# A two-block transformer kernel: the first attention's q is squared, roped and turned in another order, and six fillings of its maxima move to two slots of the attention

## Chip, cores and metric

One Trainium2 chip, one core of it. The metric is the device time of one execution in microseconds (us); the number for a kernel is the median over its runs.

## The reference, cut to what matters here

Two transformer blocks run one after the other on 256 tokens of width 1024. The change lies in the first attention of the first block ("nsa"). Cut to what that part computes:

```
h = rms_norm(x, norm_g) * (1 + scale) + shift          # scale, shift, gate from cond @ ada_w + ada_b
q, kc, vc, ks, vs, kw, vw, gl, z = split(h @ w_in)     # q: 16 heads of 64; k, v: 4 heads
q  = partial_rope(rms_norm(q, q_g), cos, sin)
ks = partial_rope(rms_norm(ks, k_g[1]), cos, sin);  kw likewise with k_g[2]
k_cmp = partial_rope(rms_norm(compress(kc, 0), k_g[0])); v_cmp = compress(vc, 1)
gates = sigmoid(gl + gate_b)
o_cmp = softmax(q k_cmp^T * s, mask) v_cmp
o_slc = softmax(q ks^T * s, mask) vs                   # 4 blocks, all selected at 256 tokens
o_win = softmax(q kw^T * s, mask) vw
o = gates0 * o_cmp + gates1 * o_slc + gates2 * o_win
x = x + gate * ((o * silu(z)) @ w_out)
```

The softmaxes subtract the row maximum, and every matrix product is in fp32 precision. The second attention ("moba"), the first block's end and the whole second block (feed-forward, two more attentions, feed-forward) aren't touched.

## The kernel before

The program is one list of instructions per engine, written by hand as Python functions: `tensor` (PE), `scalar` (ACT), `vector` (DVE), `gpsimd` (POOL) and `sync` (SP, which issues the DMAs). Engines meet through counting semaphores: an instruction ends with `then_inc(*name(key))`, and another engine does `w.wait_ge(*name.at(key))`. Each engine runs its list in order, so a wait holds up everything behind it on that engine.

**Weights.** All weights are one stream of units of 128 x 1024 fp32 (512 KB). SP fetches unit u into one of seven buffers `w_raw`, as soon as the unit seven places earlier has been used up. ACT makes the rounded part `w_hi` (line 1028, `rounds`), DVE the remainder `w_lo = w_raw - w_hi` (line 1525, `rests`); four buffers each. PE multiplies three times per block (hi by hi, hi by lo, lo by hi), in `linear` (lines 482 and 491). The units of a second kind, "ada" (modulation weights), aren't multiplied on PE: ACT scales each half by a condition value in place (line 1032, `scale_chunk`), and POOL adds the halves up (line 2285, `sum_chunk`). An ada unit's buffer comes free when POOL has added it, and then SP fetches the unit seven places on. In the stage of z the stream takes turns: one unit of z, one of ada.

**Stages around the change, in PE's order.** The linears `nsa_q0` and `nsa_q1` (q in two halves of 8 heads, four units each, banks 0 and 1), with `compress_up(0)` between them; `compress_up(1)` (line 571); `nsa_gate` (one unit, line 491, banks 0 and 1); `nsa_vsvw` (four units, line 482, banks 2 and 3); `nsa_z0` (banks 0, 1) and `nsa_z1` (banks 2, 3), four units each, line 491; then `pair_attention`.

**How q gets ready.** After the linear, ACT squares it (`head_squares`, line 1076), DVE sums the squares (`head_sums`, line 1585), POOL takes the power -1/2 (`head_power`, lines 2257 and 2260), DVE scales q out of its bank into `tokq` (`head_scales`, line 1605), and POOL ropes it (`head_ropes`, lines 2246 to 2250). PE turns it by transposes (`q_turns`, line 506: two calls of four transposes per half), and ACT and DVE place the turned q as hi and lo parts in `qs` (`q_places`, line 1032; `q_rests`, line 1778). `k_turns`, `k_places` (kh, line 1032) and `k_rests` (kl, line 1787) do the same for k. The gate's linear waits for the scaling of q1, because both use bank 0.

**Maxima.** Softmax needs each row's maximum first. A "filling" n of 24 is a set of scores in one bank (`maxima_scores`, lines 612, 614 and 617); DVE reduces the bank to row maxima `mx` (`maxima`, line 1676), and the next filling into that bank waits for that (`filling_free`). Three fillings serve two heads. They stand behind each unit of z, three at a time: 0 to 11 under z0, 12 to 23 under z1. From filling 8 on they alternate between two banks, 7 and 4. Compressed scores (line 592, 16 matmuls) stand behind the first two units of z1; DVE masks and shifts them (`compressed_shift`, lines 1937 to 1947), ACT takes exp.

**Attention.** `pair_attention` has slots i = 0 to 7 and three more. In slot i, PE does scores (i, 0), values (i-1, 1), scores (i, 1), for odd i-2 a turn of the finished heads, then `nsa_hook(i)` and values (i, 0). Scores are lines 639 to 645, values 665 to 670. DVE does `evict(i-1)` (lines 1689 to 1703, four kinds of instruction), which waits for values (i-1, 1); values (i, 0) wait for evict's third step, `parts_of_o`. Slot i needs only the maxima of its own heads.

The banks before are set by this line, and the places where the fillings stand by the two loops over z:

```
bank = (7, 4)[n % 2] if s == "nsa" and n > 7 else order[n % 4]      # order = (7, 2, 3, 4) for nsa
...
for j in linear("nsa_z1", 1, (h_hi, h_lo), h_of(0), False, [m_reduced.at(("nsa", 6))]):
    for n in range(12 + 3 * j, 15 + 3 * j):
        maxima_scores("nsa", n, filling_free("nsa", n, first))
```

Of the kernel before, what the change touches and what calls it, by code (L numbers as in the profile page):

```python
# [188 lines left out]
def program(nc, wts, cols_d, rows_d, const_d, pos_d, gate_bias_d, x_d, out_d):  # L189
# [8 lines left out]
    with ctx:  # L198
# [203 lines left out]
        for s, per, branches, order in (("nsa", 2, slice(0, 2), (7, 2, 3, 4)), ("moba", 4, slice(0, 1), (6, 7, 4, 5))):  # L402
# [56 lines left out]
        def tensor(e):  # L459
# [308 lines left out]
            whole(linear("nsa_gate", 0, (h_hi, h_lo), h_of(0), False, [hn_scaled.at(("nsa_q1", 1, 0))]))  # L768
            for j in linear("nsa_vsvw", 1, (h_hi, h_lo), h_of(0), True, [gelu_done.at((1, 1))]):
                if j == 0:  # L770
                    compress_down(1, banks[6], heads_placed.at(("nsa_kskw", 1)))
                if j == 1:
# [4 lines left out]
                    q_turns("nsa_q0", 0, banks[5], kc_placed.at())  # L777
                if j == 2:
                    q_turns("nsa_q0", 1, banks[4], gates_done.at())
            first = {0: modulated.at((0, 3)), 1: v_done.at(("nsa", 1)), 2: v_done.at(("nsa", 1)),  # L780
                     3: heads_placed.at(("nsa_q0", 1))}
            for j in linear("nsa_z0", 0, (h_hi, h_lo), h_of(0), False, [gate_biased.at()]):
                if j == 0:
                    q_turns("nsa_q1", 0, banks[6], vc_done.at(3))
                if j == 1:
                    q_turns("nsa_q1", 1, banks[5], heads_placed.at(("nsa_q0", 0)))
                for n in range(3 * j, 3 * j + 3):
                    maxima_scores("nsa", n, filling_free("nsa", n, first))
            for j in linear("nsa_z1", 1, (h_hi, h_lo), h_of(0), False, [m_reduced.at(("nsa", 6))]):
                for n in range(12 + 3 * j, 15 + 3 * j):  # L790
                    maxima_scores("nsa", n, filling_free("nsa", n, first))
                if j < 2:
                    compressed_scores(j, (banks[5], banks[6]),
                                      (c_masked.at(0) if j else heads_placed.at(("nsa_q1", 1)),))
# [7 lines left out]
            outs = [linear("nsa_out0", 1, (o_hi, o_lo), o_two("nsa"), True, [z_done.at(("nsa_z1", 1))]),  # L802
                    linear("nsa_out1", 2, (o_hi, o_lo), o_two("nsa"), True, [exped.at(("nsa", 7, 1, 1))])]

            def nsa_hook(i):
                if i == 0:
                    compressed_turns(1, banks[0], gate_row_done.at(4))
                if i == 1:
                    ada_columns(5, banks[0], pc_done.at(1))
                if i in (4, 6, 8):  # L810
# [3 lines left out]
                if i in (9, 10):  # L814
# [3 lines left out]
                           [[m_reduced.at(("nsa", 23)), c_masked.at(1)], [m_reduced.at(("nsa", 23)), pc_done.at(0)],  # L818
# [195 lines left out]
        def scalar(e):  # L1014
# [228 lines left out]
            for j, u in enumerate(of["nsa_q1"]):  # L1243
# [19 lines left out]
            for j, u in enumerate(of["nsa_vsvw"]):  # L1263
# [7 lines left out]
                if j == 2:  # L1271
                    q_places("nsa_q0", "nsa_q", 0, banks[5])
                if j == 3:
                    q_places("nsa_q0", "nsa_q", 1, banks[4])
# [3 lines left out]
            for j, u in enumerate(of["nsa_z0"]):  # L1278
                rounds(u, 4)
                if j == 1:  # L1280
                    q_places("nsa_q1", "nsa_q", 0, banks[6])
                if j == 2:
                    q_places("nsa_q1", "nsa_q", 1, banks[5])
# [229 lines left out]
        def vector(e):  # L1513
# [401 lines left out]
            for j, u in enumerate(of["nsa_vsvw"]):  # L1915
                rests(u)
                if j == 3:
                    q_rests("nsa_q0", "nsa_q", 0, banks[5])
# [47 lines left out]
            for j, u in enumerate(of["nsa_z0"]):  # L1966
                rests(u, 4)
                if j == 0:
                    q_rests("nsa_q0", "nsa_q", 1, banks[4])
                if j == 2:  # L1970
                    q_rests("nsa_q1", "nsa_q", 0, banks[6])
                if j == 3:
                    q_rests("nsa_q1", "nsa_q", 1, banks[5])
                maxima("nsa", 3 * j, 3 * j + 1, 3 * j + 2)
            for j, u in enumerate(of["nsa_z1"]):
# [4 lines left out]
                maxima("nsa", 12 + 3 * j, 13 + 3 * j, 14 + 3 * j)  # L1980
# [5 lines left out]
            def nsa_hook(i, step_):  # L1986
# [241 lines left out]
        def gpsimd(e):  # L2228
# [322 lines left out]
```

## Time and profile before

| | |
|---|---|
| median of 3 runs | 964.97 us (962.23 to 964.99) |
| the profiled execution | 962.59 us |
| its span in the trace | 960.8 us |
| mean granted clock of TensorE | 0.979 of full |
| PE busy | 902.5 us, 94% of the span |
| DVE, ACT, POOL busy | 572.7, 489.4, 175.6 us |
| the chain that ended last | PE 84%, DVE 8%, ACT 4%, issue 2%, DMA 1%, POOL 1% |
| read from HBM | 161.37 MB, 169 GB/s over the span |

PE is busy nearly all the time, so time is to be had only where PE stands idle or where its clock is granted at half. "Busy" is the share of time with at least one instruction running, and matmuls overlap, so that the start of the next is a better measure of a matmul's cost than its duration. Times in the rows are from the start of the span.

### The profile page before, as it was taken

The page shows a single profiled execution, that of the slowest core. Times are in us where ns is not written, and L with a number is a line of the kernel's source. Part 1 is how long each engine was busy: PE and PEld are TensorE (multiplying, and loading weights), DVE is VectorE, ACT ScalarE, POOL GpSimd, SP SyncE. Part 2 cuts the span into 40 slices and gives each one's busy share as a digit, 9 for nine tenths or more (in the row PEclk, how much of TensorE's full clock was granted, in tenths as well). Part 3 has the DMA queues.
Part 4 walks back from the last instruction along what each step waited for, and adds up shares of the span by engine and source line. Part 5 has one row for each costly group of instructions (what it writes and reads, how often), then busy time and mean ns, then how long its engine had stood idle before and what let it go on. Part 6 is the DMA issues. An engine that isn't in the chain of part 4 may idle for free.

```text
span 960.8 us, 12986 instructions
## 1 busy us (share of the span) xinstructions
PE 902.5 (94%) x4989; PEld 773.8 (81%) x4989; DVE 572.7 (60%) x913; ACT 489.4 (51%) x764; POOL 175.6 (18%) x192
## 2 busy tenths in 40 slices
PE   2699898999889999999999999999999999999998
PEld 2588787899678888888888888887788788888886
DVE  5974586545766637755555446676455755555542
ACT  3334573556355564645454447585664554545431
POOL 1015344355126440000000002352001100000000
PEclk9899898999899999999999999999999999999999
DMA  9855645254646245555556655544225465555650
GB/s 359 316 183 181 219 140 190 76 149 143 199 160 196 79 142 179 175 190 195 195 184 188 176 175 188 153 140 128 67 88 157 150 206 189 175 177 187 206 176 22
DMA packets 45692, 163.26 MB, mean 170 GB/s; under 512 B 5184, under 2 KB 5440, under 8 KB 45632
## 3 DMA queue, kind: packets, MB, share of 16 engines
q1 hardware_dynamic: 45632, 162.44, 52.9%
q8 instruction: 40, 0.66, 0.3%
q14 instruction: 20, 0.16, 0.1%
HBM read 161.37 MB, written 1.05 MB: 169 GB/s over the span
## 4 chain that ended last, share of the span: by engine, by line
PE 84%; DVE 8%; ACT 4%; issue 2%; DMA 1%; POOL 1%; SPq 0%; DVEq 0%; ACTq 0%
PE bank L482 57%; PE bank L491 11%; PE bank L506 4%; DVE w_lo L1525 2%; PE bank L639 2%; DVE mx L1676 1%; DVE ada_acc L1623 1%; PE bank L645 1%; DMA w_raw<-in_weights 1%; PE bank L722 1%; PE bank L665 1%; PE bank L666 1%; PE bank L667 1%; ACT kh L1032 1%; PE bank L670 1%
## 5 line engine op out<-in xcount | busy, mean ns | idle before, releaser
L1028 ACT ACTIVATE w_hi<-w_raw 128x1024 fp32r<-128x1024 f32 (+2 forms) x249 | 259.1, 1046 | 186.0 <-PE bank L482 160.3
L1525 DVE TENSOR_TENSOR w_lo<-w_raw,w_hi 128x1024 fp32r<-128x1024 f32 (+2 forms) x249 | 303.3, 1236 | 81.3 <-ACT w_hi L1028 80.6
L482 PE MATMUL bank<-w_hi,h_hi 128*128 128x512 f32 (+1 forms) x576 | 230.5, 400 | 10.7 <-ACT h_hi L1032 6.3
L482 PE MATMUL bank<-w_hi,h_lo 128*128 128x512 f32 (+1 forms) x576 | 226.1, 393 | 0.0
L482 PE MATMUL bank<-w_lo,h_hi 128*128 128x512 f32 (+1 forms) x576 | 225.5, 392 | 0.0
L482 PEld LDWEIGHTS bank<-w_hi,h_hi 128*128 128x128 f32 x576 | 110.1, 191 | 33.6 <-issue 12.5
L482 PEld LDWEIGHTS bank<-w_hi,h_lo 128*128 128x128 f32 x576 | 109.5, 190 | 23.2
L482 PEld LDWEIGHTS bank<-w_lo,h_hi 128*128 128x128 f32 x576 | 110.2, 191 | 21.3
L2285 POOL TENSOR_TENSOR ada_acc<-ada_acc,w_raw 128x512 f32<-128x512 f32 x56 | 78.2, 1396 | 99.7 <-ACT w_raw L1032 94.4
L491 PE MATMUL bank<-h_hi,w_hi 128*128 128x256 f32 x264 | 78.8, 299 | 3.7 <-DVE tokq L1605 3.1
L491 PE MATMUL bank<-h_lo,w_hi 128*128 128x256 f32 x264 | 76.2, 289 | 0.0
L491 PE MATMUL bank<-h_hi,w_lo 128*128 128x256 f32 x264 | 76.1, 288 | 0.0
L482 PE MATMUL bank<-w_hi,a_hi 128*128 128x512 f32 x176 | 70.2, 399 | 0.0
L482 PE MATMUL bank<-w_lo,a_hi 128*128 128x512 f32 x176 | 69.3, 394 | 0.0
L482 PE MATMUL bank<-w_hi,a_lo 128*128 128x512 f32 x176 | 69.2, 393 | 0.0
L2080 DVE SCALAR_TENSOR_TENSOR act<-bank,stats,act 128x256 f32<-128x256 f32 x44 | 21.1, 483 | 67.5 <-ACT act L1395 67.5
L491 PEld LDWEIGHTS bank<-h_hi,w_hi 128*128 128x128 f32 x264 | 52.1, 197 | 4.9 <-issue 4.6
L491 PEld LDWEIGHTS bank<-h_lo,w_hi 128*128 128x128 f32 x264 | 52.2, 198 | 0.4 <-issue 0.2
L491 PEld LDWEIGHTS bank<-h_hi,w_lo 128*128 128x128 f32 x264 | 52.1, 197 | 0.0
L482 PE MATMUL bank<-w_hi,qs 128*128 128x512 f32 x128 | 44.2, 416 | 2.5 <-DVE w_lo L1525 1.8
L482 PEld LDWEIGHTS bank<-w_hi,a_lo 128*128 128x128 f32 x176 | 33.0, 188 | 8.4
L482 PEld LDWEIGHTS bank<-w_hi,a_hi 128*128 128x128 f32 x176 | 33.0, 188 | 7.7
(296 smaller groups left out, 1346.4 us busy)
## 6 DMA issues: line engine op xcount, KB each, us to landing
w_raw<-in_weights SPq DMA_DIRECT2D x298, 512.0 KB, 4.2
w_raw<-in_weights SPq DMA_DIRECT2D x4, 360.0 KB, 3.2
x<-in_x SPq DMA_DIRECT2D x1, 1024.0 KB, 7.6
gate_row<-in_gate_bias SPq DMA_DIRECT2D x2, 512.0 KB, 6.4
out<-x SPq DMA_DIRECT2D x4, 256.0 KB, 3.2
w_raw<-in_weights SPq DMA_DIRECT2D x3, 256.0 KB, 2.6
const<-in_constants SPq DMA_DIRECT2D x1, 413.5 KB, 9.0
cols<-in_columns SPq DMA_DIRECT2D x1, 208.5 KB, 2.5
```

The source lines that it names most:

```text
L482: mm = e.matmul(pb[t][:, 0:n], xs[q], ws[p], start=(k + kk == 0 and i == 0), stop=(k + kk == kts - 1 and i == 2))
L491: mm = e.matmul(o, ws[p], xs[q], start=(k + kk == 0 and i == 0 and b % 2 == 0), stop=(k + kk == kts - 1 and i == 2 and (b % 2 == 1 or b == ...
L506: mm = e.transpose(bank[0:int(np.prod(src.shape[1:])), o:o + src.shape[0]], src, ident)
L639: e.matmul(o, k[:, g, br, j * P:(j + 1) * P], qs[:, ha:hb + 1:2, j * P:S], start=m == 0, stop=False, skip_group_check=True)
L645: mm = e.matmul(o[:, a, (t - j) * P:(t - j + 1) * P], bcast(mx[:, t, h, it["mx"]:it["mx"] + 1], [P, P]), minus_r[:, :], start=False, stop= ...
L665: e.matmul(o[0], p[:, a * S:a * S + P], v[0], start=True, stop=True)
L666: e.matmul(o[1], p[:, a * S + P:(a + 1) * S], v[0], start=True, stop=False)
L667: mm = e.matmul(o[1], p[:, 2 * S + a * P:2 * S + (a + 1) * P], v[1], start=False, stop=True)
L1028: e.activation(w_hi[i % NSPLIT][:, 0:c], raw[v % NRAW][:, 0:c], ACT.Copy).then_inc(*rounded(v))
L1525: e.tensor_tensor(w_lo[i % NSPLIT][:, 0:c], raw[v % NRAW][:, 0:c], w_hi[i % NSPLIT][:, 0:c].bitcast(F32), ALU.subtract).then_inc(*rested(v))
L2080: e.scalar_tensor_tensor(v, pairs[(p0 + n) % 2][tt][:, S:2 * S], norm_rs[i][:, tt:tt + 1], v, ALU.mult, ALU.mult).then_inc(*act_done((f, n ...
L2285: e.tensor_tensor(acc, acc, raw[u % NRAW][:, kk * 512:(kk + 1) * 512], ALU.add).then_inc(*ada_summed((c, k)))
```

## The change

It has five parts.

1. ACT squares q1 before it places k, and rounds the gate's weights and those behind it up to four units ahead (`rounds(u, 4)`) around that; DVE sums q1's squares before it makes k's low parts.
2. POOL ropes the second token tile of q0 before the power of q1.
3. PE turns q0 right behind the gate's linear into banks 7 and 1 (before: inside vsvw, into banks 5 and 4), and q1 inside vsvw behind its third unit into banks 5 and 7 (before: inside z0, into banks 6 and 5). The places and rests on ACT and DVE follow.
4. Fillings: 0 to 11 stay under z0 (filling 0 goes to bank 6 instead of 7, and 8 may start without waiting for another filling's reduction); 12 to 17 stand under z1, two behind each of its first three units instead of three behind each of four; 18 to 23 go to slots 2 and 3 of the attention, three in each, into banks 2 and 3.
5. Waits that name those steps are set to the new places.

```diff
-        for s, per, branches, order in (("nsa", 2, slice(0, 2), (7, 2, 3, 4)), ...
+        for s, per, branches, order in (("nsa", 2, slice(0, 2), (6, 2, 3, 4)), ...
-                bank = (7, 4)[n % 2] if s == "nsa" and n > 7 else order[n % 4]
+                bank = order[n % 4] if s == "moba" or n < 8 else (7, 4)[n % 2] if n < 18 else 2 + n % 2
...
-                    if fillings[s][m]["bank"] == fillings[s][n]["bank"]:
+                    if fillings[s][m]["bank"] == fillings[s][n]["bank"] and n not in first:
...
+            q_turns("nsa_q0", 0, banks[7], modulated.at((0, 3)))
+            q_turns("nsa_q0", 1, banks[1], hn_scaled.at(("nsa_q1", 1, 0)))
             for j in linear("nsa_vsvw", 1, (h_hi, h_lo), h_of(0), True, [gelu_done.at((1, 1))]):
...
                 if j == 2:
-                    q_turns("nsa_q0", 1, banks[4], gates_done.at())
+                    q_turns("nsa_q1", 0, banks[5], kc_placed.at())
+                    q_turns("nsa_q1", 1, banks[7], heads_placed.at(("nsa_q0", 0)))
...
             for j in linear("nsa_z1", 1, (h_hi, h_lo), h_of(0), False, [m_reduced.at(("nsa", 6))]):
-                for n in range(12 + 3 * j, 15 + 3 * j):
+                for n in range(12 + 2 * j, 14 + 2 * j) if j < 3 else ():
                     maxima_scores("nsa", n, filling_free("nsa", n, first))
...
+                if i in (2, 3):
+                    for n in range(12 + 3 * i, 15 + 3 * i):
+                        maxima_scores("nsa", n, filling_free("nsa", n, first))
...
-                if j == 3:
+            head_squares("nsa_q1", hn_summed.at(("nsa_q0", 1)))
+            for j, u in enumerate(of["cmp_w1_1"]):
+                rounds(u, 4)
+                if j == 0:
                     k_places("nsa_kskw", "nsa_ks", 0, banks[4])
                     k_places("nsa_kskw", "nsa_kw", 1, banks[6])
-            head_squares("nsa_q1", hn_summed.at(("nsa_q0", 1)))
-            for j, u in enumerate(of["cmp_w1_1"]):
-                rounds(u)
...
                 if j == 0:
+                    head_sums("nsa_q1")
+                if j == 2:
                     k_rests("nsa_kskw", "nsa_ks", 0, banks[4])
                     k_rests("nsa_kskw", "nsa_kw", 1, banks[6])
-                    head_sums("nsa_q1")
                 if j == 3:
                     head_scales("nsa_q1")
...
-                maxima("nsa", 12 + 3 * j, 13 + 3 * j, 14 + 3 * j)
+                if j < 3:
+                    maxima("nsa", 12 + 2 * j, 13 + 2 * j)
...
+                if step_ == 1 and i in (2, 3):
+                    maxima("nsa", *range(12 + 3 * i, 15 + 3 * i))
...
+            head_ropes("nsa_q0", 1)
             head_power("nsa_q1")
-            head_ropes("nsa_q0", 1)
             head_ropes("nsa_q1")
```

The order of DVE's instructions while PE does `compress_up(1)` (the remainders `w_lo`, the low parts `kl` of k, the sums into `stats` and the scaling into `tokq` of q1), with + for the change:

```order
 L1896 SCALAR_TENSOR_TENSOR kc<-bank,stats,rows 128x64
+L1585 TENSOR_REDUCE stats<-squares 128x8 x2
+L1525 TENSOR_TENSOR w_lo<-w_raw,w_hi 128x1024
 L1787 SCALAR_TENSOR_TENSOR kl<-bank,cols,kh 64x2x256 x4
-L1585 TENSOR_REDUCE stats<-squares 128x8 x2
-L1525 TENSOR_TENSOR w_lo<-w_raw,w_hi 128x1024 x2
+L1525 TENSOR_TENSOR w_lo<-w_raw,w_hi 128x1024
 L1605 TENSOR_TENSOR tokq<-bank,stats 128x512 x2
```

The sums stand ahead of kl now; the scaling of q1 still stands behind kl and behind two remainders.

PE's order in slot 2 of the attention, behind scores (2, 1) (lines 639 to 645) and ahead of values (2, 0) (from line 665):

```order
 L641 MATMUL bank<-unit_r,mask_r 128x256
 L645 MATMUL bank<-minus_r,mx 128x128 x2
+L612 MATMUL bank<-mask_r,unit_r 128x512
+L614 MATMUL bank<-kh,qs 128x256 x2
+L614 MATMUL bank<-kh,qs 128x512
+L617 MATMUL bank<-mask_r,unit_r 128x2x128
+L614 MATMUL bank<-kh,qs 128x512
+L617 MATMUL bank<-mask_r,unit_r 128x2x128
 L665 MATMUL bank<-tokv,soft_t 128x65
 L666 MATMUL bank<-tokv,soft_t 128x65
```

Three fillings (18, 19, 20) have come between; slot 3 has the same with 21, 22, 23, behind the turn of the first heads.

DVE's order in the same two slots, of the change, from evict(1) in slot 2 to evict(3) in slot 4 (line 1641 adds a bias to the gate row; 1724 and 1729 gate the turned heads and make their low part):

```order
L1689 RECIPROCAL factors<-bank 128x2x2 x2
L1692 TENSOR_TENSOR factors<-factors,gates 128x2x2 x2
L1698 TENSOR_TENSOR parts_of_o<-bank,factors 128x384 x2
L1703 TENSOR_REDUCE tokq<-parts_of_o 128x2x64 x2
L1641 TENSOR_TENSOR gate_row<-bank,gate_row 128x512
L1676 TENSOR_REDUCE mx<-bank 128x4
L1676 TENSOR_REDUCE mx<-bank 128x2 x2
...
L1724 SCALAR_TENSOR_TENSOR gated<-bank,zs 128x512
L1729 TENSOR_TENSOR qs<-gated,qs 128x2x256
L1676 TENSOR_REDUCE mx<-bank 128x4
L1676 TENSOR_REDUCE mx<-bank 128x2 x2
```

Each slot's three reductions stand behind the whole of that slot's evict, and in slot 3 behind the gating as well; before, none stood there.

## Rows read from the trace of the kernel before

**Rows 1.** The page, busy time: engine, us busy, share of the span, instructions.

```profile
PE 902.5 (94%) x4989; PEld 773.8 (81%) x4989; DVE 572.7 (60%) x913; ACT 489.4 (51%) x764; POOL 175.6 (18%) x192
```

**Rows 2.** Busy time by stretch: us, busy per engine (instructions), PEclk, DMA share, GB/s.

```profile
102.30:105.36 3.06, 0.00 (x1) 0.03 (x1) 1.44 (x3) 1.45 (x3) 2.98 (x5) 0.76 0.90 308
105.36:110.62 5.26, 5.26 (x25) 5.26 (x26) 1.12 (x1) 0.00 (x0) 3.84 (x9) 0.50 0.90 308
123.26:155.30 32.04, 27.20 (x209) 25.62 (x207) 28.15 (x38) 22.58 (x32) 19.08 (x13) 1.00 0.62 202
155.30:162.00 6.70, 6.70 (x30) 6.60 (x31) 3.52 (x7) 0.00 (x0) 1.73 (x2) 0.50 0.61 215
162.00:171.84 9.84, 8.64 (x58) 7.09 (x56) 4.88 (x9) 1.03 (x3) 0.00 (x0) 1.00 0.00 0
244.50:251.16 6.66, 6.65 (x21) 5.50 (x22) 2.29 (x3) 2.64 (x3) 0.00 (x0) 0.54 0.64 228
```

**Rows 3.** Waits, PE, 100 to 172 us: waiter <- releaser: us, times, longest.

```profile
PE bank L614 <- DVE mx L1676: 5.7, 5, 2.7
```

**Rows 4.** Timeline of PE: start, us, line, operation [idle before <- releaser].

```profile
94.75 0.39 PE L482 MATMUL bank<-w_hi,h_lo 128*128 128x512 f32 x1
...
105.36 0.55 PE L491 MATMUL bank<-h_hi,w_hi 128*128 128x256 f32 x1 [3.06 <-DVE tokq L1605]
```

**Rows 5.** Timeline of ACT, 92 to 99 us.

```profile
92.00 5.64 ACT L1032 ACTIVATE kh<-bank,cols 64x512 fp32r<-64x512 f32 x8 [5.67 <-PE bank L506]
97.66 1.08 ACT L1076 ACTIVATE squares<-bank 128x512 f32<-128x512 f32 x2
```

**Rows 6.** Timeline of DVE and POOL, 100 to 106 us.

```profile
103.92 1.29 DVE L1605 TENSOR_TENSOR tokq<-bank,stats 128x512 f32<-128x512 f32 x2 [1.67 <-POOL stats L2260]
...
100.17 3.72 POOL L2260 TENSOR_TENSOR stats<-stats 128x16 f32<-128x16 f32 x1
```

**Rows 7.** Timeline of PE: three fillings, from the first to the next linear.

```profile
135.06 0.39 PE L612 MATMUL bank<-mask_r,unit_r 128*128 128x512 f32 x1
...
136.23 0.28 PE L491 MATMUL bank<-h_hi,w_hi 128*128 128x256 f32 x1
```

**Rows 8.** Timeline of PE: the two longest waits for a reduction.

```profile
141.81 0.50 PE L614 MATMUL bank<-kh,qs 128*128 128x512 f32 x1 [1.75 <-DVE mx L1676]
...
155.30 0.80 PE L614 MATMUL bank<-kh,qs 128*128 128x512 f32 x1 [2.67 <-DVE mx L1676]
```

**Rows 9.** Timeline of DVE under z: three reductions, and remainders alone and beside POOL.

```profile
136.33 1.89 DVE L1676 TENSOR_REDUCE mx<-bank 128x4 fp32r<-128x512 f32 x3
138.25 1.23 DVE L1525 TENSOR_TENSOR w_lo<-w_raw,w_hi 128x1024 fp32r<-128x1024 f32 x1
...
152.35 2.30 DVE L1525 TENSOR_TENSOR w_lo<-w_raw,w_hi 128x1024 fp32r<-128x1024 f32 x1
```

**Rows 10.** Timeline of ACT: the rounding of z1's third unit.

```profile
141.24 1.06 ACT L1028 ACTIVATE w_hi<-w_raw 128x1024 fp32r<-128x1024 f32 x1 [2.31 <-DMA w_raw<-in_weights]
```

**Rows 11.** Timeline of DVE in the attention: evict(1), gate row; gating and low part.

```profile
189.46 0.25 DVE L1689 RECIPROCAL factors<-bank 128x4 f32<-128x4 f32 x2 [3.19 <-PE bank L670]
...
191.23 1.09 DVE L1703 TENSOR_REDUCE tokq<-parts_of_o 128x128 f32<-128x384 f32 x2
192.25 0.68 DVE L1641 TENSOR_TENSOR gate_row<-bank,gate_row 128x512 f32<-128x512 f32 x1
...
199.30 0.68 DVE L1724 SCALAR_TENSOR_TENSOR gated<-bank,zs 128x512 f32<-128x512 f32 x1
200.68 0.69 DVE L1729 TENSOR_TENSOR qs<-gated,qs 128x512 fp32r<-128x512 f32 x1 [0.70 <-ACT qs L1032]
```

**Rows 12.** Timeline of PE: values (2, 0) and (3, 0) begin; a later wait.

```profile
191.25 0.44 PE L665 MATMUL bank<-tokv,soft_t 128*128 128x65 f32 x2 [0.23 <-DVE parts_of_o L1698]
...
198.54 0.33 PE L665 MATMUL bank<-tokv,soft_t 128*128 128x65 f32 x2
...
244.51 0.77 PE L482 MATMUL bank<-w_hi,qs 128*128 128x512 f32 x1 [1.82 <-DVE w_lo L1525]
```

More of the change, by code:

```diff
@@ L401, in program @@
         fillings, slots = {"nsa": [], "moba": []}, {"nsa": [], "moba": []}
-        for s, per, branches, order in (("nsa", 2, slice(0, 2), (7, 2, 3, 4)), ("moba", 4, slice(0, 1), (6, 7, 4, 5))):
+        for s, per, branches, order in (("nsa", 2, slice(0, 2), (6, 2, 3, 4)), ("moba", 4, slice(0, 1), (6, 7, 4, 5))):
             nb = branches.stop
@@ L776, in tensor @@
                                     for tt in range(TT)]).then_inc(*gates_turned())
-                    q_turns("nsa_q0", 0, banks[5], kc_placed.at())
                 if j == 2:
-                    q_turns("nsa_q0", 1, banks[4], gates_done.at())
[L780 to L786, printed above, removed]
+                    q_turns("nsa_q1", 0, banks[5], kc_placed.at())
+                    q_turns("nsa_q1", 1, banks[7], heads_placed.at(("nsa_q0", 0)))
+            first = {0: vc_done.at(3), 1: v_done.at(("nsa", 1)), 2: v_done.at(("nsa", 1)), 3: gates_done.at(),
+                     8: heads_placed.at(("nsa_q1", 1)), 18: z_done.at(("nsa_z1", 1)), 19: z_done.at(("nsa_z1", 1))}
+            for j in linear("nsa_z0", 0, (h_hi, h_lo), h_of(0), False, [gate_biased.at(), heads_placed.at(("nsa_q0", 1))]):
                 for n in range(3 * j, 3 * j + 3):
@@ L793, in tensor @@
                     compressed_scores(j, (banks[5], banks[6]),
-                                      (c_masked.at(0) if j else heads_placed.at(("nsa_q1", 1)),))
+                                      (c_masked.at(0) if j else m_reduced.at(("nsa", 7)),))
                 if j == 2:
@@ L801, in tensor @@
             o_two = lambda s: lambda k: [o_rounded.at((s, k // 2)), o_rested.at((s, k // 2))]
-            outs = [linear("nsa_out0", 1, (o_hi, o_lo), o_two("nsa"), True, [z_done.at(("nsa_z1", 1))]),
+            outs = [linear("nsa_out0", 1, (o_hi, o_lo), o_two("nsa"), True, [z_done.at(("nsa_z1", 1)), m_reduced.at(("nsa", 23))]),
                     linear("nsa_out1", 2, (o_hi, o_lo), o_two("nsa"), True, [exped.at(("nsa", 7, 1, 1))])]
@@ L817, in tensor @@
             pair_attention("nsa", [v_done.at(("nsa", 1)), pc_done.at(1), zeroed.at(3)],
-                           [[m_reduced.at(("nsa", 23)), c_masked.at(1)], [m_reduced.at(("nsa", 23)), pc_done.at(0)],
+                           [[m_reduced.at(("nsa", 17)), c_masked.at(1)], [m_reduced.at(("nsa", 17)), pc_done.at(0)],
                             lambda pr: ada_cols.at(5 + pr) if pr else gate_row_done.at(5)], nsa_hook)
@@ L1270, in scalar @@
                         copy(vc[gs, g, :], banks[6][gs, 0:HD]).then_inc(*vc_done(g))
-                if j == 2:
-                    q_places("nsa_q0", "nsa_q", 0, banks[5])
+                if j == 0:
+                    q_places("nsa_q0", "nsa_q", 0, banks[7])
+                    q_places("nsa_q0", "nsa_q", 1, banks[1])
                 if j == 3:
-                    q_places("nsa_q0", "nsa_q", 1, banks[4])
+                    q_places("nsa_q1", "nsa_q", 0, banks[5])
             for tt in range(TT):
@@ L1279, in scalar @@
                 rounds(u, 4)
[L1280 to L1283, printed above, removed]
+                if j == 0:
+                    q_places("nsa_q1", "nsa_q", 1, banks[7])
                 scale_chunk(4, j)
@@ L1916, in vector @@
                 rests(u)
+                if j in (0, 1):
+                    q_rests("nsa_q0", "nsa_q", j, banks[(7, 1)[j]])
                 if j == 3:
-                    q_rests("nsa_q0", "nsa_q", 0, banks[5])
+                    q_rests("nsa_q1", "nsa_q", 0, banks[5])
                 if j == 2:
@@ L1968, in vector @@
                 if j == 0:
[L1969 to L1973, printed above, removed]
+                    q_rests("nsa_q1", "nsa_q", 1, banks[7])
                 maxima("nsa", 3 * j, 3 * j + 1, 3 * j + 2)
```

## Prediction

> **What bounds the kernel now.** I read the page's busy times first, then the waits of PE, then busy time by stretch with the granted clock, and last the timelines of each engine around the stages that the change touches. PE is busy 94% of the span [rows 1], so a change of order can gain only where PE stands idle or runs at half clock. Three such places lie near the change. Between compress_up(1) and the gate's linear PE waits 3.06 us for q1's scaling [rows 4], and the linear then runs at a granted clock of 0.50 (the lower level, 1.2 GHz) [rows 2]. Under z, from 123.26 to 171.84 us, PE waits 5.7 us in five waits for reductions of maxima [rows 3], the longest 1.75 and 2.67 us [rows 8]. Right behind the 2.67 us wait the clock is 0.50 for 6.7 us [rows 2]. DVE is the reason: it is busy 28.15 of 32.04 us between 123.26 and 155.30 [rows 2]. It has slack in the attention, where it waits 3.19 us before evict(1) [rows 11].
>
> **The head part (squares, sums, kl).** ACT waits 5.67 us idle for k's turn and then places kh until 97.64 us; q1's squares follow at 97.66 [rows 5]. q1's last matmul ends at 94.75 + 0.39 = 95.14 [rows 4], so with the squares first they end near 95.2 + 0.54 = 95.7 instead of 98.74. The power needs 3.72 us on POOL [rows 6]; with the sums it is done near 100.6 instead of 103.9. POOL's ropes of q0 that now stand ahead of it fit into its earlier idle time. But DVE's scaling stands behind kl and behind two remainders, and these wait for ACT: squares to 95.7, one rounding of 1.06 [rows 10], kh in 5.64 [rows 5] to 102.5, one rounding to 103.5, its remainder 1.23 [rows 9] to 104.8. The scaling (1.29) ends at 106.1, before at 103.92 + 1.29 = 105.2 [rows 6]. So PE is let go 0.9 us later, not earlier. PE runs at half clock there anyway, and where that stretch ends by time and not by work, up to half of the delay comes back: +0.5 to +0.9, I take **+0.7**. The roundings moved ahead of gelu(1) have the whole gate's linear (5.26 us [rows 2]) as cover; without that they would cost their 1.06 us. The DMA issues keep their order; v's third unit is fetched when compress_up(1) has used its first unit, in time for its later rounding.
>
> **Turns of q.** The sixteen transposes are as many as before and only change places on PE: 0. ACT and DVE now do q1's places and rests largely before z0 ends its first unit; in vsvw their cover is PE's four units. The wait added on z0 (q0's second half placed) falls some 6 us before z0 by this schedule: 0.
>
> **Under z.** (a) Six fillings leave. Three take 136.23 - 135.06 = 1.17 us of PE [rows 7]: 2 x 1.17 = **-2.3**. (b) DVE loses six reductions here (1.89 us for three, so 3.8 us [rows 9]) and half of q's rests. From the starts of the units, the reductions of fillings 0 to 10 and 12 to 17 are then done before PE asks. Filling 11 still follows the reduction of filling 9 in the same bank with only filling 10 between: 0.5 us stays. 5.7 - 0.5 = **-5.2** (between 0, if something else makes DVE late, and -5.7). What could be late next is z1's weights: an ada unit is scaled, added and replaced by the unit of z1, and the rounding of z1's third unit waited 2.31 us for its DMA until 141.24 [rows 10]. In the new order that comes 1 to 2 us later, PE needs it near 152: cover enough. (c) With no wait above a microsecond left, the half clock behind the 2.67 us wait goes: 6.7 us at 0.50 [rows 2] did 3.35 us of work, **-3.4**. Together -10.9.
>
> **In the attention.** DVE has time there, but the fillings stand on PE between scores and values. In slot 2, PE ends scores (2, 1) at 191.02 (values at 191.25 after 0.23 idle [rows 12]) and does fillings 18 and 19 in some 0.8 us. Filling 20 shares bank 2 with 18, so it waits for the reduction of 18. That reduction stands behind evict(1) (189.46 to 192.32) and the gate row (to 192.93) [rows 11], and ends, with 0.69, near 193.6. Values (2, 0) follow at 194.0 instead of 191.25: **+2.75**, of which 1.8 us is idle. In slot 3, filling 23 waits for 21, whose reduction stands behind evict(2), the gating (199.30) and the low part (to 201.37) [rows 11]; it ends near 202.06, the filling 0.4 later, and values (3, 0) start at 202.5 instead of 198.54 [rows 12]: **+3.95**, some 2.5 us idle. Later slots keep their pace, since slots 4 to 7 need the moved maxima long after. Together +6.7.
>
> **The clock in the attention.** The trace shows one wait of 1.82 us (at 244.51 [rows 12]) that is followed by a clock of 0.54 over 6.66 us [rows 2], one of 2.67 that is too, and one of 1.75 [rows 8] inside a stretch at 1.00. The new waits of 1.8 and 2.5 us lie in that region. A low stretch of 3.4 to 6.8 us costs half of itself, 1.7 to 3.4; none or two are possible. I take one, at **+2.5**. The Trainium skill, page "TensorE: Matmul & The Clock Gate", section "Why this matters for your kernels", would let gaps as short as these pass without a drop in clock; by it nothing is added here, and the sum would be 959.1. The trace speaks against it with the 1.82 us wait.
>
> **The sum.** 0.7 - 10.9 + 6.7 = -3.5, and with one low stretch -1.0. Against the profiled execution's 962.59 (span 960.8, 1.8 around it) that is 961.6 (959.1 without the stretch). The profiled execution is 2.4 us under the median of 964.97 and inside the runs' 962.23 to 964.99; this spread is as large as one low stretch more or less, so I keep the sum against 962.59. A difference of 0.3%, 2.9 us, is about what a measurement of this kernel can tell from none: faster is below 962.1, slower above 967.9.
>
> **The rivals.**
> 1. *Both new waits pass without a low stretch.* For it: 1.75 us passed once. Against it: 1.82 and 2.67 did not. 959.1.
> 2. *Both trip the clock.* For it: the same rows; slots 2 and 3 are over 7 us apart, so each can have its own. -3.5 + 2 x 2.5 = +1.5: 964.1, no change to be measured.
> 3. *The head part gains what its squares gain.* If the scaling weren't held by kl and the remainders, PE would be let go at most 1.8 us earlier, because kh took that long to pass in part. Against it: the order on DVE. It would be -3.5 - 0.7 - 1.8 + 2.5: 959.1 with one stretch, 956.6 with none.
> 4. *The waits are moved, not removed: slower.* The place is DVE and the weights' chain under z. If POOL's additions stretch the remainders there (2.30 us instead of 1.23 [rows 9]) and z1's weights come late, DVE stays behind PE and the 5.7 us remain, while the attention pays its 6.7 and two low stretches of 3.4. 0.7 - 2.3 - 3.4 + 6.7 + 6.8 = +8.5: 971. It decides once less than about 1 us of the 5.2 is gained and both waits trip. Against it: 3.8 us of reductions leave DVE there, more than its largest lateness.
> 5. *The change doesn't do what it says*, in that DVE's reductions of the moved fillings don't hold PE (one reduction would be free before evict). The order contradicts it; then the attention would cost 2.3 and the time be 954.7. I give it 0.03.
>
> **How the numbers follow.** My forecast, one low stretch, 961.6: 0.40. Rival 1: 0.22. Rival 2: 0.15. Rival 3: 0.07. Rival 4: 0.13. Rival 5: 0.03. The forecast lies only 0.5 us inside "faster", so a little under half of its chance goes to "same". Faster: 0.22 of the forecast, 0.20 of rival 1, 0.06 and 0.03 of rivals 3 and 5, less a little for what they may lack: 0.47. Same: 0.18 and 0.15, and some of rival 4's milder forms: 0.39. Slower: 0.14. The range runs from 956.5 (rival 3 without a stretch) to 966.5 (rival 2 with stretches of full length, 965.9, and half a microsecond); it leaves out rivals 4 and 5. Where signs divide, the likeliest case's own range is 959.9 to 963.4, for stretches of one to two microseconds more or less.
>
> **What would show it.** In the new profile: squares of q1 at about 95.2, the gate's linear starting near 106.2 (earlier than 105.4: the head step is wrong); no wait over 1 us and a clock of 1.00 from the gate's end to the attention; scores (0, 0) near 161.6 instead of 171.84; in slots 2 and 3 one wait each of PE for a reduction, near 1.8 and 2.5 us; and a clock below 1.00 once behind them. The sum is wrong if scores (0, 0) start after 164, or if a slot's added time is under 1.5 or over 5 us.

## The result and the profile after

The changed kernel takes 969.78 us (median of 4 runs, 969.53 to 971.11), the kernel before beside it 963.6 us (4 runs, 961.65 to 964.99). The ratio is 1.0068, with a 95% interval of 1.0053 to 1.0083: slower, where 961.6 us and no more than 966.5 had been forecast. In a second set it took 971.88 us against 961.7, ratio 1.0109 (1.0083 to 1.0136). Its profiled execution took 971.11 us, 8.5 more than the one of before, with a span of 969.3 us.

The page's busy times, as [rows 1] before. PE is busy 9.7 us longer, though its work is the same 4989 matmuls:

```profile
PE 912.2 (94%) x4989; PEld 784.0 (81%) x4989; DVE 573.6 (59%) x913; ACT 489.9 (51%) x764; POOL 180.3 (19%) x192
```

The waits of PE from 95 to 265 us (waiter <- releaser: us, times, longest), against [rows 3] and the 3.06 us of [rows 4]:

```profile
PE bank L614 <- DVE mx L1676: 4.0, 3, 1.9
PE bank L491 <- DVE tokq L1605: 3.8, 1, 3.8
```

The timeline of PE at the marks of the prediction: the gate's linear, the one wait left under z, scores (0, 0), filling 20 and values (2, 0), filling 23 and values (3, 0), and the later wait of [rows 12]:

```profile
107.86 0.55 PE L491 MATMUL bank<-h_hi,w_hi 128*128 128x256 f32 x1 [3.75 <-DVE tokq L1605]
...
142.73 0.50 PE L614 MATMUL bank<-kh,qs 128*128 128x512 f32 x1 [0.52 <-DVE mx L1676]
...
161.79 0.50 PE L639 MATMUL bank<-qs,kh 128*128 128x512 f32 x1
...
183.53 0.50 PE L614 MATMUL bank<-kh,qs 128*128 128x512 f32 x1 [1.68 <-DVE mx L1676]
...
183.98 0.41 PE L665 MATMUL bank<-tokv,soft_t 128*128 128x65 f32 x2
...
200.41 0.50 PE L614 MATMUL bank<-kh,qs 128*128 128x512 f32 x1 [1.85 <-DVE mx L1676]
...
200.86 0.33 PE L665 MATMUL bank<-tokv,soft_t 128*128 128x65 f32 x2
...
253.24 0.76 PE L482 MATMUL bank<-w_hi,qs 128*128 128x512 f32 x1 [1.82 <-DVE w_lo L1525]
```

In this execution everything from the first linears on lies 1.82 us later than in the profile of before (compress_up(1) starts at 96.80 instead of 94.98). The change moves nothing of PE there, so 1.82 is taken off below wherever a time is compared with one of before. Scores (0, 0) then start at 159.97 instead of 171.84: 11.9 us have been won. From there to the later wait it takes 253.24 - 161.79 = 91.45 us, before 244.51 - 171.84 = 72.67: 18.8 us have been lost.

Where they went is in the column of the granted clock in busy time by stretch (columns as in [rows 2], the clock third from the right), for the stage under z and then the slots 2 and 3:

```profile
126.29:161.79 35.50, 34.98 (x273) 33.43 (x271) 30.85 (x44) 21.84 (x32) 21.05 (x14) 1.00 0.64 213
...
180.70:184.10 3.40, 1.72 (x12) 1.31 (x12) 3.34 (x6) 3.40 (x7) 1.27 (x1) 1.00 0.54 154
184.10:197.74 13.64, 13.64 (x62) 13.25 (x61) 3.37 (x10) 2.66 (x5) 2.54 (x2) 0.50 0.26 78
197.74:201.15 3.41, 1.56 (x11) 1.15 (x10) 2.60 (x5) 2.75 (x5) 1.29 (x2) 1.00 0.00 0
201.15:214.80 13.65, 13.65 (x59) 12.97 (x59) 4.94 (x10) 2.29 (x5) 4.60 (x3) 0.50 0.32 116
214.80:221.00 6.20, 6.20 (x46) 5.71 (x45) 0.16 (x1) 3.14 (x5) 1.52 (x2) 1.00 0.01 3
```

Under z the clock is 1.00 and PE nearly never idle. In the attention, the clock falls to 0.50 (1.2 GHz) within 0.8 us of the end of each of the two new waits, and stays there for 13.65 us while PE is busy all the time. At half clock 13.65 us do 6.8 us of work, so each stretch costs 6.8 us. PE's busy time grows for the same reason: slower matmuls, not more of them.

### The profile page after: what moved, and what is told of

Read it like the earlier page. It is cut to its first block, busy times and chain, and to the rows that moved or that the text cites. A ratio compares the mean times of both kernels' runs of the same rounds, so it can differ in the third digit from the quotient of the medians.

```text
span 969.3 us, 12985 instructions
## 1 busy us (share of the span) xinstructions
PE 912.2 (94%) x4989; PEld 784.0 (81%) x4989; DVE 573.6 (59%) x913; ACT 489.9 (51%) x764; POOL 180.3 (19%) x192
## 4 chain that ended last, share of the span: by engine, by line
PE 86%; DVE 6%; ACT 5%; issue 2%; DMA 1%; POOL 0%; SPq 0%; DVEq 0%; ACTq 0%; POOLq 0%
PE bank L482 57%; PE bank L491 11%; PE bank L506 4%; PE bank L639 2%; DVE w_lo L1525 2%; PE bank L645 1%; DMA w_raw<-in_weights 1%; DVE ada_acc L1623 1%; ACT w_hi L1029 1%; PE bank L667 1%; PE bank L666 1%; PE bank L665 1%; PE bank L722 1%; PE bank L670 1%; ACT kh L1033 1%
## 5 line engine op out<-in xcount | busy, mean ns | idle before, releaser
L482 PEld LDWEIGHTS bank<-w_hi,h_hi 128*128 128x128 f32 x576 | 110.0, 191 | 33.6 <-issue 12.5
```

The costliest lines, as they stand in the source:

```text
L482: mm = e.matmul(pb[t][:, 0:n], xs[q], ws[p], start=(k + kk == 0 and i == 0), stop=(k + kk == kts - 1 and i == 2))
```

## The experiments

The runs were made in three sets, each on one chip. The kernel before took 963.03 us beside the first (`busy_wait`, `head_only`, `fills_only`, `split_slot`), 961.7 beside the second (`wait_alone`, `busy_slot3`, `changed_again`, `fills_again`) and 961.17 beside the third (the two shifts, `split_again`, `split_head`). A ratio is always against the kernel before of the same set. Only one execution of each run has a trace; of the others the time and the mean granted clock over the span are on record. The two traced executions of the changed kernel, each with two stretches of 13.65 us at half clock in the attention, have a mean clock of 0.972 and 0.965; that of `busy_wait`, with none there, has 0.986.

**Waits filled with work.** `busy_wait` computes fillings 19 and 22 six times over, so that PE works where it had waited:

```diff
-                for j, (o, q, k) in enumerate(f["items"]):
+                for _ in range(6 if s == "nsa" and n in (19, 22) else 1):
+                    for j, (o, q, k) in enumerate(f["items"]):
```

> The changed kernel, with fillings 19 and 22 computed six times over into their own banks (same result), 5 x 0.35 us of matmuls each, which lie in the two waits of slots 2 and 3. Theory 1 (the waits of 1.68 and 1.85 us let the clock fall for 13.65 us each, and that is where 13.6 us go): with PE busy in the waits both low stretches vanish, and the time falls from about 970 to 957. Rival A (the attention's own kind of matmuls holds the clock down once it is low, or the new place of the work does it, whatever PE does in the waits): the stretches stay, 970 to 972. Rival B (not the clock, but the waits themselves and the added work are the loss): unchanged to +1, 970 to 971.

957.73 us (ratio to before 0.9948, 0.9931 to 0.9964): 12 us less than the changed kernel, with more work on PE. In slots 2 and 3 one wait of 0.8 us is left, and the clock in its trace stays at 1.00 through them:

```profile
125.00:200.00 75.00, 73.11 (x558) 68.54 (x557) 51.76 (x91) 44.07 (x73) 39.59 (x28) 1.00 0.48 152
200.00:216.00 16.00, 16.00 (x123) 15.12 (x123) 7.28 (x20) 8.03 (x15) 4.56 (x5) 1.00 0.43 145
```

The waits were filled with about as much work as they had been long, so little can have been gained by their going. What has gone is the half clock, and with it 12 us.

**The waits alone.** `wait_alone` is the kernel before with its order, plus two bare waits of PE ahead of values (2, 0) and (3, 0):

```diff
+                if i == 2:
+                    w.wait_ge(*gate_row_done.at(5))
+                if i == 3:
+                    w.wait_ge(*o_rounded.at(("nsa", 0)))
```

> The kernel before, with its order of instructions kept, and on TensorE alone two added waits: in slot 2 it stands until DVE is done with row 5 of the gates, in slot 3 until the first rounding of the slot before is there (from the rows before, about 2 us each). No filling and no turn is moved, and all that the reference asks is computed. Theory 1 (a wait of near 2 us in slots 2 and 3 is what takes the clock to half, for 13.65 us each time, whatever brought the wait): 963.0 + 4 of waits + 13.6 of clock = 980.6 us, with two stretches of 13.65 us at half clock in the attention. Rival (the waits cost only themselves, and the clock fell in the changed kernel from another thing, such as the changed head or the work that now lies under z): 967 us and no stretch at half clock behind the two waits.

975.85 us (974.48 to 977.62), ratio 1.015 (1.0116 to 1.0184). The waits are 1.93 and 1.44 us long:

```profile
192.80 0.69 PE L665 MATMUL bank<-tokv,soft_t 128*128 128x65 f32 x2 [1.93 <-DVE gate_row L1645]
...
207.93 0.44 PE L665 MATMUL bank<-tokv,soft_t 128*128 128x65 f32 x2 [1.44 <-ACT qs L1036]
```

and the stretches that go with them are 13.66 and 10.24 us long. The first begins 0.35 us before its wait ends, the second 1.6 us after its own has ended:

```profile
192.45:206.11 13.66, 13.31 (x59) 12.93 (x60) 2.90 (x9) 4.02 (x8) 3.82 (x3) 0.50 0.29 81
206.11:209.52 3.41, 1.97 (x16) 1.73 (x16) 2.30 (x3) 2.44 (x5) 0.95 (x1) 1.00 0.00 0
209.52:219.76 10.24, 10.24 (x45) 9.84 (x45) 2.83 (x9) 2.53 (x6) 5.16 (x4) 0.50 0.48 154
```

By those lengths the sum would be 961.7 + 3.4 + (13.66 + 10.24) / 2 = 977.1; 975.85 were measured, and 965 is what the waits alone would give. The 980.6 expected took both waits and the second stretch too long. Fillings, turns and head are not needed for the loss: two waits of 1.4 to 1.9 us in these slots are enough.

**One wait filled.** `busy_slot3` repeats filling 22 alone.

> The changed kernel, with filling 22 of slot 3 computed six times over so that TensorE is busy where it had waited; slot 2 keeps its wait. Nothing is left out of the computation. Theory 1 (each wait has its own stretch at half clock, 13.65 us long, 6.8 us dear): slot 3's stretch goes, slot 2's stays, 969.8 - 6.8 = 963 us, with one stretch at half clock in the attention. Rival (the first fall brings the second, so that one is as good as two or none as good as one): with slot 2's stretch still there the second comes all the same, 969 to 971 us.

963.05 us (957.56 to 965.75, ten executions), ratio 1.0015 (0.9996 to 1.0033). The trace has slot 2's stretch and no other:

```profile
182.61:196.27 13.66, 13.66 (x62) 13.27 (x61) 3.33 (x10) 2.68 (x5) 2.54 (x2) 0.50 0.25 78
196.27:215.00 18.73, 18.61 (x138) 17.18 (x137) 7.82 (x15) 9.15 (x16) 9.09 (x7) 1.00 0.30 102
```

Each wait has its own stretch, and the second isn't brought by the first. One of the ten executions took 957.56 us at a mean clock of 0.989, against 0.975 to 0.980 in the others: it probably had no stretch at all, though its wait was in the program too.

**Half of the change: the head alone.** `head_only` is the changed kernel with fillings 12 to 23 back under z1, three behind each unit, as before.

> The changed kernel, with fillings 12 to 23 back under z1, three per unit. Theory 1: attention as before, no low stretch there; under z the wait of 1.75 us falls to 0.5, the later ones of 2.67 us and less stay with their half clock, and the gate's linear starts 0.9 us later: 962 to 964. Rival C (the head part costs): 966 or more.

961.1 us (958.65 to 962.85) against 963.03, ratio 0.9978 (0.9962 to 0.9993): a little under the 962 to 964 expected, and rival C is refuted. Five waits for reductions remain under z, though shorter (3.5 us in all, the longest 1.4), and so does the half clock:

```profile
PE bank L491 <- DVE tokq L1602: 3.8, 1, 3.8
PE bank L614 <- DVE mx L1673: 3.5, 5, 1.4
```

```profile
147.50:154.60 7.10, 7.10 (x36) 7.10 (x36) 4.98 (x9) 5.16 (x9) 5.83 (x5) 0.52 0.84 276
```

The head's own wait is 3.8 us, as in the changed kernel and 0.7 more than before. The waits under z are shorter probably because q's last rests now leave DVE before these reductions; that wasn't tried by itself.

**The other half: the fillings alone.** `fills_only` is the kernel before with nothing but the six fillings moved (banks, places on PE, reductions on DVE).

> The kernel before, with the move of the six fillings alone (head part, turns and ropes as before). Theory 1: under z it gains most of what the change gains (2.3 of work, 3.4 of clock, some 4 of waits), and the attention loses the same 19 us as in the changed kernel (13.6 clock, 3.3 waits, 2.3 work): 963.6 - 9.7 + 19 = about 973. Rival C (the head part is what costs): under 966.

959.69 us against 963.03, ratio 0.998 (0.9953 to 1.0007): missed, by 13 us. Seven executions took 958 to 960.4 us, one 963.82 and one 968.52; the traced one took 3150.64 us, isn't counted and can't be used, so the kernel was run again for its trace:

> The kernel before with the six fillings moved and nothing else, a second time, for its trace: it had taken 959.7 us where 973 was expected. Theory 1 (waits of near 2 us in slots 2 and 3 bring the half clock): then its waits there must be shorter than 1.7 us or absent, 959 to 960 us, no stretch at half clock in slots 2 and 3. Rival (its waits are as long as the changed kernel's, and the clock fell there only in some executions, by where the waits lie): 959 to 969 us, waits of 1.6 us and over in the trace with a granted clock of 1.00 behind them.

This time the median is 967.73 us, ratio 1.0035 (1.0005 to 1.0065), 8 us more than in the first set: the same program lay on one chip mostly low and on the other mostly high. The ten executions took 959.11 to 969.85 us, in two groups: three at 959 to 961 with a mean clock of 0.982 to 0.986, and seven at 966 to 970 with 0.972 to 0.980. The profiled one (960.32 us) is among the fast. It has the waits, 1.68 us in slot 2 and even 2.51 in slot 3, and the clock behind both is 1.00:

```profile
184.26 0.50 PE L614 MATMUL bank<-kh,qs 128*128 128x512 f32 x1 [1.68 <-DVE mx L1679]
...
195.39 0.50 PE L614 MATMUL bank<-kh,qs 128*128 128x512 f32 x1 [2.51 <-DVE mx L1679]
```

```profile
184.01:190.84 6.83, 6.58 (x53) 6.37 (x54) 2.21 (x8) 2.42 (x4) 3.31 (x3) 1.00 0.49 153
...
195.40:205.00 9.60, 9.60 (x69) 8.94 (x70) 5.57 (x11) 2.87 (x6) 5.18 (x4) 1.00 0.46 165
```

So the length of a wait doesn't settle it: the same 1.68 us is followed by half clock in the changed kernel and by full clock here. The rival held, and so did its range.

**The changed kernel again**, beside these:

> The changed kernel as it is, beside the others of this set. Theory 1: 969.8 us, two stretches of 13.65 us at half clock behind the waits of 1.7 and 1.85 us. Rival (whether the clock falls behind such a wait is a matter of where it lies against something else that the program does not set): executions of one kernel differ by 6 to 14 us, and a stretch is missing in some profile.

971.88 us (971.23 to 972.9), with waits of 1.68 and 1.73 us and the two stretches of 13.65 us. All eight executions of the changed kernel, in two sets, lie between 969.5 and 972.9 us with a mean clock of 0.965 to 0.972. Two of them have a trace and show both stretches; by time and clock the other six had them too. One thing that differs from the fillings alone is where the waits lie: slot 2's ends 86.7 and 86.9 us after the start of compress_up(1) in the two traces, and 87.5 us after it in `fills_again`.

**The attention moved as a whole.** To try that, filling 13, ahead of the attention, is computed three or five times over, 0.9 or 1.8 us of added work:

```diff
+                for _ in range(3 if s == "nsa" and n == 13 else 1):
```

> The changed kernel with filling 13, under z1, computed three times over: nothing is left out, and PE gets some 0.9 us more work ahead of the attention, so that all of the attention, with both waits, comes 0.9 us later and is otherwise the same. Theory P (whether the clock falls behind a wait of 1.7 to 1.9 us hangs on where in the execution the wait lies, as the kernel with the fillings alone suggests: there waits of 1.68 and 2.51 us were followed by a clock of 1.00): the waits are as long as in the changed kernel but one or both of the long stretches are gone in most executions, 957 us (970 + 0.9 - 13.6), or 964 with one. Rival (the length of the wait alone decides): both stretches stay, 971 us.

> As the one with 0.9 us, but filling 13 is computed five times over, some 1.8 us of added PE work ahead of the attention. Theory P (the place decides): one or both stretches gone in most executions, 958 us, or 965 with one. Rival (length alone): both stretches, 972 us.

960.45 us (959.12 to 970.05, ten executions), ratio 1.0004 (0.9979 to 1.003), and 961.13 us (958.58 to 965.75, ten), ratio 0.9996 (0.9975 to 1.0016). With 0.9 us added, six of ten took 959.1 to 961.0 at a mean clock of 0.982 to 0.987, three 963 to 965.2 at 0.977 to 0.981, and one 970.05 at 0.968. That is the profiled one. It has waits of 1.68 and 1.95 us and both stretches:

```profile
95.32 3.67 PE L571 MATMUL bank<-zs,w_raw 128*128 128x60 f32 x32
...
182.78 0.65 PE L615 MATMUL bank<-kh,qs 128*128 128x512 f32 x1 [1.68 <-DVE mx L1677]
...
199.76 0.58 PE L615 MATMUL bank<-kh,qs 128*128 128x512 f32 x1 [1.95 <-DVE mx L1677]
```

```profile
182.98:196.63 13.65, 13.65 (x61) 13.16 (x61) 3.64 (x10) 2.91 (x6) 2.83 (x3) 0.50 0.24 78
200.04:213.70 13.66, 13.66 (x60) 13.09 (x60) 5.11 (x11) 2.75 (x6) 4.91 (x4) 0.50 0.32 116
```

With 1.8 us, the profiled execution (964.82) has none behind slot 2's 1.68 us and one of 10.24 us that begins 2 us after the end of slot 3's 2.51:

```profile
184.99 0.50 PE L615 MATMUL bank<-kh,qs 128*128 128x512 f32 x1 [1.68 <-DVE mx L1677]
...
196.12 0.50 PE L615 MATMUL bank<-kh,qs 128*128 128x512 f32 x1 [2.51 <-DVE mx L1677]
```

```profile
184.50:191.00 6.50, 6.01 (x48) 5.84 (x49) 1.96 (x5) 2.66 (x5) 3.54 (x3) 1.00 0.51 159
...
198.17:208.41 10.24, 10.24 (x46) 9.86 (x45) 3.64 (x9) 1.93 (x4) 3.33 (x2) 0.50 0.42 154
```

Added work of 0.9 us makes the kernel some 10 us faster, and in nine of ten executions at least one of the stretches is gone, if time and clock are the sign of it. So a small shift changes how often the clock falls behind the same waits. But the place within the program isn't what decides by itself: here slot 2's wait of 1.68 us ends 182.78 - 95.32 = 87.5 us after the start of compress_up(1) and the clock falls, and in `fills_again` the same wait ends as far behind it, at 87.5 us, and the clock stays at 1.00. What else decides, and what in the chip the place of a wait would have to be measured against, wasn't worked out here; nor why the changed kernel meets both falls each time.

**The waits removed by order.** `split_slot` moves the first two fillings of slots 2 and 3 (18, 19 and 21, 22; the new hook `early`) ahead of values (i-1, 1), and their reductions ahead of evict, so that filling 20 (23) finds its bank free:

```diff
+                    early(i)
                     if 0 < i <= n:
                         values(i - 1, 1)
...
+                    if s == "nsa" and i in (2, 3):
+                        maxima("nsa", 12 + 3 * i, 13 + 3 * i)
                     if 0 < i <= n:
                         evict(i - 1)
...
-                    maxima("nsa", *range(12 + 3 * i, 15 + 3 * i))
+                    maxima("nsa", 14 + 3 * i)
```

> The changed kernel, with fillings 18, 19 (slot 2) and 21, 22 (slot 3) ahead of values (i-1, 1) and their reductions ahead of evict(i-1); filling 20 or 23 stays where it is. No filling has to wait for a reduction behind evict. Theory 1: no wait over 0.5 us in slots 2 and 3, no low stretch there: 969.8 - 13.6 (clock) - 3.5 (waits) = about 953. Rival A (the work in the attention brings the clock down even without a wait): 965 or more. Rival B (DVE is the bound in these slots, so the wait comes back at values): 955 to 960 with waits for evict.

> The changed kernel, with fillings 18, 19 and 21, 22 ahead of values (i-1, 1) in slots 2 and 3 and their reductions ahead of evict, a second time, with more rounds: 954 us, no wait above 1 us in slots 2 and 3 and a clock of 1.00 there in all executions. If its 954 was by luck of where the waits fall, some executions are above 960.

954.06 us (four executions), and 954.14 us with five rounds (952.11 to 955.28, ratio 0.9915, 0.9891 to 0.9939). No execution is above 960, as expected. From the trace of the second: the low stretch that goes with the head's wait is still there, the attention is clean.

```profile
106.23:113.06 6.83, 4.52 (x21) 4.55 (x22) 3.42 (x4) 2.16 (x5) 3.91 (x8) 0.50 0.87 303
...
172.00:215.00 43.00, 43.00 (x336) 40.71 (x336) 26.06 (x59) 23.94 (x45) 23.51 (x17) 1.00 0.45 143
```

**The head mended too.** `split_head` adds one step, DVE's scaling of q1 ahead of kl:

```diff
                 if j == 2:
+                    head_scales("nsa_q1")
                     k_rests("nsa_kskw", "nsa_ks", 0, banks[4])
                     k_rests("nsa_kskw", "nsa_kw", 1, banks[6])
-                if j == 3:
-                    head_scales("nsa_q1")
```

> The same with one more step: on DVE the scaling of q1 stands ahead of kl (behind compress_up(1)'s third unit, not its fourth). In the trace of the split version PE waits 3.76 us for that scaling, which ends near 106.5; with POOL's power done at 101.3 it can end near 102.6, and PE be free at 102.86. Theory (my head step: kl and the remainders hold the scaling): the wait of 3.76 us goes, and with it the stretch at half clock behind it, 954 - 3.7 - 3.4 = 947 us; 950 if the clock falls there all the same. Rival (kl, moved behind the scaling, makes something else late: the gate's remainder or k's banks): a wait of 2 us and over comes back within the gate's linear, 952 to 955 us.

948.68 us (946.33 to 950.06), ratio 0.9858 (0.9832 to 0.9884): the best version, 12.5 us faster than before, and 5.5 faster than the split alone. The timelines of DVE and PE, and the clock:

```profile
101.83 1.29 DVE L1610 TENSOR_TENSOR tokq<-bank,stats 128x512 f32<-128x512 f32 x2 [2.82 <-POOL stats L2268]
103.03 3.09 DVE L1794 SCALAR_TENSOR_TENSOR kl<-bank,cols,kh 64x512 fp32r<-64x512 f32 x4
```

```profile
96.01 3.67 PE L571 MATMUL bank<-zs,w_raw 128*128 128x60 f32 x32
...
102.93 0.39 PE L571 MATMUL bank<-zs,w_raw 128*128 128x60 f32 x2
103.26 0.36 PE L491 MATMUL bank<-h_hi,w_hi 128*128 128x256 f32 x1
```

```profile
103.20:113.00 9.80, 9.57 (x60) 8.45 (x59) 8.90 (x12) 7.56 (x13) 2.36 (x7) 1.00 0.86 300
113.00:172.00 59.00, 57.88 (x429) 53.79 (x428) 44.77 (x72) 38.46 (x64) 28.13 (x20) 1.00 0.53 174
172.00:215.00 43.00, 43.00 (x335) 40.89 (x333) 23.63 (x55) 23.20 (x43) 22.51 (x17) 1.00 0.46 147
```

The gate's linear follows compress_up(1) without a wait, and its clock is 1.00. By the trace of `split_again` the wait of 3.75 us and half of the 4.52 us that PE was busy in its low stretch, 2.3, could be gained; the 3.4 expected for the clock counted the time in which PE stood still. kl now ends some 2 us later than in the split version, and holds nobody: only one wait of 0.2 us for a remainder is new.

## Why the prediction was wrong, step by step

- **The head part: right.** The second of q1's squares starts at 97.00 - 1.82 = 95.18 (forecast about 95.2), the gate's linear at 107.86 - 1.82 = 106.04; forecast 106.2, before 105.36. kl and the remainders do hold the scaling: in the trace of after the last kl starts at 104.09, and the scaling at 106.43 follows a remainder. `split_head` shows the other side of it: rival 3 of the prediction named what earlier squares are worth once the order on DVE is mended, but let PE go at most 1.8 us earlier than before and gave the clock nothing. There the gate's linear starts 103.26 - 96.01 = 7.25 us after compress_up(1), before 105.36 - 94.98 = 10.38: 3.1 us earlier. Against the order with kl first the gain is 5.5 us, the half clock included.
- **Turns of q: nearly right.** With the 1.82 us taken off, z0 starts 1.2 us later: 0.7 from the head and 0.5 between the gate's linear and z0. Eight transposes more stand there now, which adds 0.9 us, and the low stretch at the gate covers 0.9 us less of PE's work, which gives 0.4 back. The prediction put this step at nothing; under z the transposes that left give their time back.
- **Under z: right, a little small.** From z0's start to scores (0, 0): 161.79 - 126.29 = 35.50 us, before 48.58. That is -13.1 against the -10.9 forecast. PE's idle time went from 48.58 - 42.53 = 6.05 to 0.52 us (-5.5; the waits for reductions from 5.7 to 0.52, as predicted), the half clock went (-3.4), and so did the six fillings' work (-2.3) and q1's transposes (0.7 us by the starts in the trace of before); 1.2 us are left that I can't assign. Rival 4 (the waits stay under z) is refuted, though its total of 971 was nearly hit: right number, wrong mechanism. Its sum also took off the 3.4 us of clock while it kept the waits that bring that stretch.
- **In the attention: right.** Slot 2 waits 1.68 us (forecast 1.8). Slot 3 waits 1.85 us (forecast 2.5). It waits 2.51 us in the two traces in which no clock falls in slot 2 (the fillings alone and the 1.8 us shift) and 1.73 to 1.95 in the three in which it does, so the half clock, which makes PE later against DVE, is the likely reason. With 2.3 us for the fillings the step is +5.9 instead of +6.7.
- **The clock in the attention: the step that failed.** I took one low stretch of 3.4 to 6.8 us, +2.5. There were two, each of 13.65 us, +13.6. The number of stretches was rival 2's, at a chance of 0.15; the price of one was mis-sized by both, because I took the length from stretches elsewhere (6.8 us, [rows 2]) as the upper bound, for a place where the trace of before had none. This term alone is 13.6 - 2.5 = 11.1 us off, more than the whole miss of 971.11 - 961.6 = 9.5 us; the other steps and the later start come to about -1.5 together (+1.8 start, +0.5 turns, -2.2 under z, -0.8 waits and fillings in the slots, and less than 1 us behind them).

The account of the two profiled executions: start +1.8, head +0.7, z0's start +0.5, under z -13.1, slots 2 and 3 with their clock +18.8, and after the later wait -0.2: +8.5 us, from 962.59 to 971.11. The lost 18.8 are 3.5 of waits, 2.3 of fillings and 13.6 of clock, less 0.6 us that isn't assigned. The wait of 1.82 us of [rows 12] was good evidence that such a wait can bring the fall, and the 1.75 us of [rows 8] that it needn't; both are borne out.

The Trainium skill, page "TensorE: Matmul & The Clock Gate", section "Why this matters for your kernels", asks only that no gap between bursts of matmuls exceed about 3 us. By that the new waits would have cost no clock, and 959.1 was the prediction's sum for it. Waits of 1.44 to 1.93 us went with half clock here, so the measurement decides against the page. It agrees in that the kernel without the head's gap of 3.75 us and without the two new waits (`split_head`) runs at 1.00 from 103 to 215 us.

## What to carry to other kernels

Moving work off a crowded stage is only half of a change: where it lands, look for the first buffer that is reused and what stands ahead of its release on the other engine. In these slots a wait of TensorE of 1.4 to 1.9 us cost 5 to 7 us more through the clock, some four times itself, and waits of 1.68 and 2.51 us cost nothing more in another execution. So price such a wait at nothing and at its worst, with the longest stretch that a trace of the same kind of stage shows and not one from elsewhere, and remove it by order rather than trust the place. Where a wait can't be removed, repeating cheap work in it is a quick way to tell how much of its price is the clock's; here that alone made the changed kernel faster than the one before (957.73 against 963.03 us).

## What the runs showed of the hardware

- In slots 2 and 3 half clock lasted 10.24 or 13.65 us each time, with PE busy for at least 97% of it (`wait_alone`, 13.31 of 13.66), while the stretch that goes with the head's wait of 3.75 us lasts 6.83 us and begins inside the wait (`split_again`, PE busy for 4.52 of it). A longer wait didn't bring the longer stretch. Why it takes longer here to come back to 2.4 GHz wasn't tried.
- The fall doesn't come at a fixed distance from the wait: 0.35 us before the wait's end (`wait_alone`, slot 2), 0.6 and 0.7 us after it (the changed kernel), 1.6 us (`wait_alone`, slot 3) and 2 us after it (`shift_18`, slot 3), with PE busy between the wait's end and the fall.
- Executions of one program on one chip differ in it. `fills_again` has no fall in the attention in its trace (960.32 us, mean clock 0.986) and executions up to 969.85 us at 0.972; `shift_09` has both in its trace (970.05 us, 0.968) and executions down to 959.12 us at 0.982. By the same signs the changed kernel had both in all eight. A spread of 10 us is here a sign of waits that are followed by half clock in some executions only; the versions without waits in these slots spread by 2 to 4 us. A small spread doesn't show that none is there: the changed kernel's is under 2 us in each set.
- Two waits within one attention each had their own fall: filling one of them took 8.8 us off (971.88 to 963.05, one set), filling both 12 us (969.78 to 957.73, two sets).
